# Sample attention and tail of a hybrid decoder kernel: serial loads, a second piece gathered ahead, two operands of the tail reloaded earlier

## The reference, cut to what matters

```
past_sel = gather_pages(cache_sel_kv, page_table)      # 8 samples x 2048 rows of k and v, 2 groups x 64
o_nsa = nsa_core(q, pos, cmp_kv, sel_kv, win_kv, ...)  # compressed, selected (top 16 blocks), window of 512
o_mem = mem_attend(qm, mem_kv)                         # 4 heads x 128 over 256 memory tokens
gates = sigmoid(g_br).reshape(B, T, 3, D_MODEL)        # g_br = columns of u @ w_in
merged = (gates[:, :, 0] * (o_nsa @ w_br_nsa) + gates[:, :, 1] * (o_gdn @ w_br_gdn)
          + gates[:, :, 2] * (o_mem @ w_br_mem))
h = x + merged @ w_out                                 # then the MLP on h
```

## Time and profile before

| | us |
|---|---|
| median of three runs | 1646.32 |
| lowest, highest | 1644.48, 1654.56 |
| the profiled execution's own time | 1644.59 |
| its span | 1642.8 |
| PE busy | 1453.0 (88%) |
| DVE busy | 871.7 (53%) |
| ACT busy | 384.5 (23%) |
| POOL busy | 82.1 (5%) |
| mean granted clock of PE | 0.929 |

### The profile page before, as it was taken

The page is one execution under the profiler, slowest core; times in us unless marked ns, Lnnn a source line. Parts: engine busy times, 40 slices in busy tenths (PEclk is TensorE's granted clock), DMA queues, the critical chain, the costliest instruction groups (busy, mean ns, idle before and its releaser), DMA issues. The chain is left out here.

```text
span 1642.8 us, 27036 instructions
## 1 busy us (share of the span) xinstructions
PE 1453.0 (88%) x11343; PEld 1335.0 (81%) x11343; DVE 871.7 (53%) x1590; ACT 384.5 (23%) x891; POOL 82.1 (5%) x76
## 2 busy tenths in 40 slices
PE   6999899889968788989475689999989999999998
PEld 5778789789957676878343489899988999999998
DVE  3555256747633565664233345545746746465563
ACT  3543023222233344554121221000003101000000
POOL 1000001100011111110100000000000000000000
PEclk8999999999968797999578789999999999999999
DMA  9232035251321000000538073323240332323221
GB/s 350 70 119 96 16 91 184 60 196 56 119 53 52 0 2 0 2 1 1 228 138 305 28 244 90 116 81 94 97 155 26 104 103 78 103 77 102 89 91 53
DMA packets 115648, 159.03 MB, mean 97 GB/s; under 512 B 6039, under 2 KB 106839, under 8 KB 112778
## 3 DMA queue, kind: packets, MB, share of 16 engines
q1 hardware_dynamic: 111886, 122.76, 23.4%
q0 software_dynamic: 2304, 33.56, 5.1%
q10 hardware_dynamic: 1348, 1.12, 0.2%
HBM read 145.04 MB, written 16.66 MB: 98 GB/s over the span
## 5 line engine op out<-in xcount | busy, mean ns | idle before, releaser
L330 PE MATMUL ps<-uH,wh 128*128 128x260 f32 x576 | 165.8, 288 | 12.3 <-DVE wt L301 9.0
L330 PE MATMUL ps<-hH,wh 128*128 128x260 f32 x512 | 145.3, 284 | 2.6 <-DVE hT L301 2.6
L330 PE MATMUL ps<-mergedH,wh 128*128 128x260 f32 x512 | 145.4, 284 | 0.0
L330 PE MATMUL ps<-hT,wh 128*128 128x260 f32 x512 | 145.3, 284 | 0.0
L330 PE MATMUL ps<-hH,wl 128*128 128x260 f32 x512 | 144.9, 283 | 0.0
L330 PE MATMUL ps<-mergedT,wh 128*128 128x260 f32 x512 | 144.7, 283 | 0.0
L330 PE MATMUL ps<-mergedH,wl 128*128 128x260 f32 x512 | 144.4, 282 | 0.0
L457 PE MATMUL ps<-XT,w 128*128 128x256 f32 (+1 forms) x512 | 125.5, 386 | 6.3 <-DVE XT L520 6.0
L330 PEld LDWEIGHTS ps<-uH,wh 128*128 128x128 f32 x576 | 109.9, 191 | 15.2 <-DVE wt L301 9.2
L330 PE MATMUL ps<-uL,wh 128*128 128x260 f32 x384 | 109.3, 285 | 0.0
L330 PE MATMUL ps<-uH,tw 128*128 128x260 f32 x384 | 109.0, 284 | 0.0
(11 more groups left out here) (520 smaller groups left out, 3437.1 us busy)
## 6 DMA issues: line engine op xcount, KB each, us to landing
wt<-in_w_ff SPq DMA_DIRECT2D x32, 1024.0 KB, 5.4
wt<-in_w_in SPq DMA_DIRECT2D x15, 1024.0 KB, 5.8
tw<-in_w_in SPq DMA_DIRECT2D x12, 1024.0 KB, 5.4
ring<-in_cache_mem_kv SPq DMA_DIRECT2D x4, 2048.0 KB, 25.0
w<-in_cmp_w SPq DMA_DIRECT2D x8, 512.0 KB, 6.3
ring<-in_cache_win_kv SPq DMA_DIRECT2D x2, 2048.0 KB, 19.5
out_s_win<-in_cache_win_kv SPq DMA_DIRECT2D x1, 4088.0 KB
scratch_uhigh<-uH SPq DMA_DIRECT2D x1, 2080.0 KB
```

Of the source, the lines that this page charges most:

```text
L330: ins = pe.matmul(out, lhsT(i, c), rhs(j, c), start=(first and c == 0 and k == 0), stop=(last and c == chunks - 1 and k == 2))
```

## The change

Four edits:

1. Sample 1's selected piece is gathered during the prompt mixers too, into `graw` (`self.ring_filled` becomes 2), on POOL behind the last group's "tv" on PE and "sc" on DVE. `graw` becomes slot 1 of the ring.
2. SP's window load and memory keys' load each wait until the piece before them in the order of use has landed (`wait_piece(sp, k - 1)`); the memory values' load does not.
3. When the second selected job has signalled `v_done`, SP reloads `uH`, `uL` and the tail's first weight tile `tw0` into slots 0, 2 and 3 of the ring, which are next to one another. The tail no longer loads them.
4. In the tail START becomes 5.0 instead of 13.0 and the first split's key 0.1 instead of 6.5, and the places of `tw1` and `s_S0` change.

```
@@ -1508,10 +1508,10 @@
 
         assert SEQ // 64 <= 16 and SEQ <= WIN
         nc, I, O, ps, proj = self.nc, self.I, self.O, self.ps, self.proj
-        self.ring_filled = 1
+        self.ring_filled = 2
         self.qmpad = self.sb_high("qmpad", [P, NB, MH, 32])
         self.compress_setup()
-        self.ring = [self.view("w1", [P, PAGES * 256], F32)]
+        self.ring = [self.view(x, [P, PAGES * 256], F32) for x in ("w1", "graw")]
         self.filled = [self.sem(f"e_slot{k}") for k in range(7)]
         XT, HT = self.sb("XT", [P, 4, SEQ // 2]), self.sb("HT", [P, 2, 2, PCMP])
         kc = self.sb("kcp", [P, NG, 32])
@@ -1807,6 +1807,10 @@
                 yield 42
                 pool.wait_ge(self.hid_ready, hid0 + 2)
                 self.gather_piece(pool, 0, 0)
+                yield self.delta_key(TT - 1, 2.5)
+                self.d_pe.wait(pool, "tv", TT - 1)
+                self.d_dve.wait(pool, "sc", TT - 1)
+                self.gather_piece(pool, 1, 1)
 
             @block.gpsimd
             def _(pool):
@@ -1822,7 +1826,9 @@
                 sp.dma_start(O["p_state"][0].rearrange("h k v -> k h v"), self.d["state"][:, :, :]).then_inc(stored, 16)
                 sp.wait_ge(stored, 16)
         self.free("w2", "hbias", "XT", "HT", "kcp", "vcp", "sc", "cs", "Pb0", "Pb1", "PTb0", "nm", "rs", "rg",
-                  "memhl", "qmT", "kmT", "mem_kv", "graw", *self.d_names)
+                  "memhl", "qmT", "kmT", "mem_kv", *self.d_names)
+        at, _ = self.taken.pop("graw")
+        self.taken["ring1"] = (at, at + PAGES * 256)
 
 
     def gather_piece(self, pool, b, n):
@@ -1857,6 +1863,14 @@
         sm, st = self.sb("sm", [P, 8]), self.sb("st", [P, 4])
         osb = [self.sb(f"osb{i}", [P, 512]) for i in range(2)]
         obr = ring[4][0:NB, 0:3 * NH * HD].rearrange("b (i c) -> b i c", i=3)
+        a, b = self.taken["w1"][0], self.taken["ring3"][1]
+        assert b - a == 3 * PAGES * 256 and self.taken["ring2"][0] == self.taken["w1"][1]
+        for name, n in (("uH", KC * NT), ("uL", KC * NT), ("tw0", KC * WCOLS)):
+            self.taken[name] = (a, a + n)
+            a += n
+        assert a <= b
+        self.uH, self.uL = (self.view(x, [P, KC, NT], F32R) for x in ("uH", "uL"))
+        self.tw0, self.u_back = self.view("tw0", [P, KC, WCOLS], F32), self.sem("t_u_back")
         scr = {n: nc.dram_tensor("scratch_" + n, (NB, 32, w), F32, kind="Internal").ap()
                for n, w in (("cmp", P), ("sel", P), ("win", P), ("mem", 512))}
 
@@ -2092,12 +2106,19 @@
                     if what == "sel":
                         continue
                     load_free(sp, k)
+                    if what != "memv":
+                        wait_piece(sp, k - 1)
                     if what == "win":
                         src = I["cache_win_kv"][4 * r:4 * r + 4].rearrange("b (t p) v g d -> p (b t) (v g d)", p=P)
                     else:
                         src = I["cache_mem_kv"][4 * r:4 * r + 4, :, 0 if what == "memk" else 1].rearrange("b (t p) h d -> p (b t) (h d)", p=P)
                     sp.dma_start(slot(k).rearrange("p (a c) -> p a c", a=src.shape[1]), src).then_inc(fetched[k % RING], 16)
 
+                sp.wait_ge(v_done, max(n for n, (br, _) in enumerate(jobs) if br == "sel") + 1)
+                for x, dram in zip((self.uH, self.uL), self.u_dram):
+                    sp.dma_start(x.bitcast(F32)[:, :, :], dram).then_inc(self.u_back, 16)
+                w0 = self.merge_tiles()[0][0][0]
+                sp.dma_start(self.tw0[:, :, :], w0.rearrange("(c p) n -> p c n", p=P)).then_inc(self.w_loaded[self.issued % 2], 16)
                 sp.wait_ge(c_scr, 16 * R4)
                 for k in range(2):
                     sp.wait_ge(o_scr[k], 16 * ((NJ - 1 + 1 - k) // 2))
@@ -2291,14 +2312,13 @@
         ident, cTs, acc, u0 = self.C("ident"), self.cTs, self.acc, self.units
         HB = GH * NB
         self.oH, self.oL = oH, oL = self.sbr("oH", [P, 3, 4, NT]), self.sbr("oL", [P, 3, 4, NT])
-        self.uH, self.uL = self.sbr("uH", [P, KC, NT]), self.sbr("uL", [P, KC, NT])
-        S0 = self.sb("s_S0", [P, GH, NB, P])
-        raw = [self.sb_high(f"tw{i}", [P, KC, W]) for i in range(3)]
+        raw = [self.tw0, self.sb("tw1", [P, KC, W]), self.sb_high("tw2", [P, KC, W])]
         low = [self.view(f"tw{i}", [P, KC, W], F32R) for i in range(3)]
         for i in range(2):
             self.sb_high(f"wh{i}", [P, KC, W])
         self.wh = [self.view(f"wh{i}", [P, KC, W], F32R) for i in range(2)]
         sig, prod2 = self.sb_high("sig", [P, 2, WM, NT]), self.sb_high("m_prod", [P, 2, HALF])
+        S0 = self.sb_high("s_S0", [P, GH, NB, P])
         at, _ = self.taken["proj"]
         self.taken["mergedT"], self.taken["mergedH"] = (at, at + KC * NT), (at + KC * NT, at + 2 * KC * NT)
         assert 2 * KC * NT <= TT * TOKCOLS
@@ -2330,7 +2350,7 @@
         tiles = [(gates if kind == "gate" else branches)[q] for kind, q in seq] + [(srcs, KC) for srcs in self.out_tiles()[0:2]]
         NT_, k0 = len(seq), self.issued
         assert k0 == self.splits == self.tiles
-        START = 13.0
+        START = 5.0
         start = [START]
         for kind, _ in seq:
             start.append(start[-1] + NU * (2.87 if kind == "gate" else 1.44))
@@ -2353,7 +2373,7 @@
 
         S = self.local_sem
         gated, taken, added = (S("m_" + x) for x in ("gated", "taken", "added"))
-        turned, oH_kept, oL_kept, u_back = (S("t_" + x) for x in ("turned", "oH_kept", "oL_kept", "u_back"))
+        turned, oH_kept, oL_kept = (S("t_" + x) for x in ("turned", "oH_kept", "oL_kept"))
         s_in, stored = S("s_in"), S("s_stored")
         p = Steps(S("s_pe"), ["sums", "bc", "qk", "read", "rows", "orow"] + [f"add{i}" for i in range(8)])
         a = Steps(S("s_act"), ["eg", "rt", "rows", "sqo", "ro"])
@@ -2377,9 +2397,6 @@
 
                 def loads():
                     yield 0.0
-                    load(0)
-                    for x, dram in zip((self.uH, self.uL), self.u_dram):
-                        sp.dma_start(x.bitcast(F32)[:, :, :], dram).then_inc(u_back, 16)
                     load(1)
                     for h in range(GH):
                         sp.dma_start(S0[:, h], I["state_gdn"][:, h].rearrange("b k v -> k b v")).then_inc(s_in, 16)
@@ -2411,7 +2428,7 @@
                             if i == 0:
                                 pe.wait_ge(self.w_split, k + 1)
                                 if n == 0:
-                                    pe.wait_ge(u_back, 32)
+                                    pe.wait_ge(self.u_back, 32)
                                 if kind == "branch" and q == 0:
                                     pe.wait_ge(oL_kept, EARLY)
                                 if kind == "branch" and q == BP:
@@ -2529,7 +2546,7 @@
                     self.high_low(dve, cut(raw[n % 3]), cut(self.wh[k % 2]), cut(low[n % 3]), self.w_high, k + 1).then_inc(self.w_split, 1)
 
                 def splits():
-                    yield 6.5
+                    yield 0.1
                     split(0)
                     for n in range(1, NT_ + 1):
                         yield start[n - 1] + 0.2
```

5 lines of the change are left out of this document (3 added, 2 removed).

## The result

Twenty runs of the changed kernel have a median of 1641.54 us (1634.36 to 1647.53), twenty of the kernel before 1650.74 (1644.48 to 1661.07): a ratio of 0.9939, 95% interval [0.9923, 0.9955]. The change is a gain of 0.6%, some 9 to 10 us. The forecast was 16.9 us off one profiled execution of 1644.59 us, 1628, with a range up to 1637. The measured median lies above that range.

A forecast was written before the change was run, and what follows sets the result against it. PE was taken as the bound, 88% busy, with waits for gathers in sample attention and for `uL` in the tail. Savings of 10.1 + 1.8 + 5.0 = 16.9 us off 1644.6 gave 1627.7, stated as 1628; range 1620 to 1637.

The forecast's parts named there:

- the base: Whole kernel: the one profiled execution, 1644.6 us, from which the summed gain was taken; median of runs put 1.7 above it.
- First job: Sample attention, first selected job: a piece gathered ahead and no loads beside the gathers save 10.1 us; bounds 5.2 and 11.1.
- Second job: Sample attention, second selected job: without the window load beside the gathers the last piece comes 1.8 us sooner; lower bound nothing.
- Rival C: Second selected job: engines serve both queues in turn, equal shares, so 5.2 us saved instead of 1.8; 1624.3; chance 0.08.
- rival D: Sample attention: each serial window or memory load comes late, 30.1 us lost against 16.9 won; 1657.8; chance 0.04.
- POOL's cover: Prompt mixers: the early gather's 0.94 us issue fits POOL's 18.08 us gap, costing nothing; 1.2 us if the cover were gone.
- one us in hand: End of sample attention: the reload ends at 932.4, read-backs went at 933.43, so no cost; bound a 2.6 us loss.
- The tail: Tail: the gate product starts earlier, without waiting for `uL`, saving 5.0 us; bounds nothing and 7.9.
- Rival B: Tail: the split at the head holds DVE and other work waits, so the tail gives nothing; 1632.7; chance 0.18.

The follow-up runs named there:

- after_again: An unchanged copy of the changed kernel, profiled and timed again: 1635.4 us, ratio to the kernel before 0.9900.
- no_ahead: The changed kernel without the second piece gathered in the mixers; serial loads and changed tail kept: 1641.5 us, ratio to the kernel before 0.9945.
- no_serial: The changed kernel with window and memory loads no longer waiting for the piece ahead of them: 1640.9 us, ratio to the kernel before 0.9928.
- win_early: The late_split kernel with the window load released by the selected job's third piece instead of the fourth: 1635.6 us, ratio to the kernel before 0.9897.
- before_again: An unchanged copy of the kernel before, profiled and timed again: 1650.3 us, ratio 0.9988.
- tail_only: The kernel before with only the changed tail and the reload; no early gather, no serial waits: 1647.5 us, ratio 0.9983.
- after_third: Another unchanged copy of the changed kernel: 1642.5 us, ratio to the kernel before 0.9935.
- late_split: The changed kernel with DVE's first gate-weight split behind the sample step's first operations and the third small product behind the first gate unit: 1635.5 us, ratio to before 0.9884.

## Why the prediction was wrong

**The sum's parts**, by the stages' means (before: two profiles, changed: three): g1 to g2 9.5 us, g2 to T 0.1, T to the end 3.4, together 12.9; forecast 16.9. So the terms were too large by 4 us, and the base was 6 us too low.

**The base is the step that failed most.** The prediction took 16.9 us off "the profiled execution", 1644.6, and set the median "1.7 above it", from three runs, without adding even these 1.7. Twenty runs put it 6.1 above. That execution had mixers of 341.7 us, where thirteen profiles reach to 352.8, and the difference goes with TensorE's clock. The whole mixers in the kernel before and in the changed kernel:

```profile
456.42:798.08 341.66, 282.29 (x1968) 247.62 (x1970) 183.31 (x434) 139.69 (x331) 47.62 (x39) 0.85 0.05 14
456.34:808.72 352.38, 293.66 (x1969) 257.01 (x1970) 183.08 (x434) 139.74 (x331) 48.50 (x40) 0.81 0.06 20
```

PE is busy 11.4 us longer at the lower clock, and stands idle as long: in all thirteen profiles the idle time of PE in the mixers is between 58.7 and 60.2 us, whatever their length. From 1650.7 the same sum gives 1633.8, still 7.7 us below the measured median. Why the clock differs between executions of one program no run shows. The account of the miss is 6.1 us of base, 4.0 of terms, and 3.7 between the stages' 12.9 and the medians' 9.2, less 0.3 of rounding: 13.5, the distance from 1628 to 1641.5. Of the 3.7 the pooled runs leave 1.7 with an uncertainty as large. Whether the early gather costs the mixers a part of that stays open: nine profiles with it have a mean of 348.6 us, four without it 346.5, and single profiles spread over 11.

**First job: 8.6 us, forecast 10.1.** The prediction reckoned 1.6 us to the first byte and then bytes at 401 GB/s, with PE starting at the last one. The trace shows a third stretch of time at the end. Windows of after_again, in which the first gather is issued at 801.95 and PE starts on the fourth piece at 815.58:

```profile
812.95:813.95 1.00, 0.18 (x1) 0.00 (x0) 0.69 (x1) 0.00 (x0) 0.00 (x0) 0.50 1.04 439
813.95:814.95 1.00, 0.00 (x0) 0.00 (x0) 0.00 (x0) 0.00 (x0) 0.00 (x0) 0.50 0.51 181
814.95:815.95 1.00, 0.37 (x2) 0.37 (x3) 0.00 (x0) 0.00 (x0) 0.00 (x0) 0.50 0.03 9
```

At the full rate the bytes would have been through at 814.4, 1.2 us ahead of PE. They are not: 256 of the 288 packets of two gathers have 16 KB (4.19 MB in all; the other 32 have 4 bytes, one for each engine and gather), and the 16 engines don't end together. The windows count a packet where it starts. Here are the gathers' packets that start from 814.38 on, in 814.5 to 814.6 (the last one of 16 KB), and from 814.6 to PE's start:

```profile
q0 software_dynamic: 11, 0.03, 6.8%
```

```profile
q0 software_dynamic: 1, 0.02, 38.2%
```

```profile
q0 software_dynamic: 7, 0.00, 0.4%
```

38.2% of 16 engines for 0.1 us is 0.61 us, so the last large packet, which starts at 814.55, ends at 815.16, and PE starts 0.42 us behind it. The end of a gather is thus some 0.8 us in which ever fewer engines still work, and 0.4 us from the last byte to PE. With 1.3 us for both, 1.6 at the start and 5.2 a piece, two pieces give 13.3 us, three 18.6, four 23.8; measured were 13.3 to 13.8, 19.0 (no_ahead), and 23.4 to 23.8. The Trainium skill, "DMA: Bandwidth & Descriptors", section "Anatomy of one DMA — SWDGE (gpsimd) path", gives a transfer's fixed cost as about 2 us and puts most of it behind the last byte, in the wait until that is confirmed as landed. The trace agrees in the sum, 1.7 us from the issue to the first packet and 0.4 from the last packet's end to PE, but not in where it lies.

The term was two: a piece ahead, forecast 5.2 and measured 5.3, and the loads kept away, forecast 4.9 and measured 3.2 to 3.4 (no_serial, no_ahead against before). Another 0.9 us came unasked between the fourth piece and g2: PE's clock is back at full between 16 and 20 us behind g1 (a mean of 0.86 over those four), before only at 28. Over the stretch from the fourth piece to g2 the mean clock was 0.78 before (35.1 us, of which 7.8 are lost by it) and 0.80 now (34.3 us, 6.9 lost), which is the 0.9. That the clock comes back sooner because the pauses in front of the pieces are fewer is not shown.

**Second job: 0.45 us, forecast 1.8.** The prediction counted 0.70 MB of loads ahead of the last piece. 0.13 MB of them were ACT's writes of small results, which stay. The DMA queues of the kernel before (packets, MB, share of 16 engines; q0 are the gathers, q1 SP's loads), from the first gather's issue to PE's start, and in the last 1.3 us of that:

```profile
q0 software_dynamic: 576, 8.39, 85.7%
q1 hardware_dynamic: 610, 0.62, 7.3%
```

```profile
q1 hardware_dynamic: 439, 0.45, 98.6%
q0 software_dynamic: 9, 0.02, 3.3%
```

Of 0.62 MB of loads 0.45 moved in these 1.3 us, on engines that were done with their part of the gathers (the last large packet ends at 879.20, 0.48 us ahead of PE). They held up next to nothing. Ahead were 0.17 MB, 0.43 us at 401 GB/s, close to the measured gain.

**Rival C was the right rule with the wrong weight.** It wanted equal shares and was said to agree with the trace "only if the gathers' packets are far larger than the loads'". They are: 16 KB against 1.0 KB. The queues of the kernel before in 804 to 816 us, with the loads beside the first job's gathers, and in 873.3 to 877.4 us, with the window load beside the second's:

```profile
q0 software_dynamic: 318, 4.69, 91.4%
q1 hardware_dynamic: 319, 0.33, 7.6%
```

```profile
q0 software_dynamic: 98, 1.57, 89.4%
q1 hardware_dynamic: 96, 0.10, 6.7%
```

The engines take turns: one packet of a load for one of a gather, which leaves the loads 6 to 7% of the two queues' bytes. That is why win_early cost almost nothing, and why the loads that move beside the first job's gathers are a small part of its 3.2 us. The Trainium skill, "DMA: Bandwidth & Descriptors", section "Queues, rings and completion order", says that each engine goes round the queues it has work for, a packet from each. The runs agree with it, one for one in the packets of the profile.

**Then why do the loads cost 3.2 us in the first job?** They are issued 0.7 us ahead of the gathers. The queues of no_serial in 809 to 814 us (the first gather is issued at 809.36), and from 814 to PE's start on the fourth piece, 826.3:

```profile
q1 hardware_dynamic: 1288, 1.32, 80.6%
```

```profile
q0 software_dynamic: 288, 4.19, 80.4%
q1 hardware_dynamic: 779, 0.81, 18.6%
```

Not one gathered packet moves in the first 4.6 us. In after_again, where nothing is ahead, the first one moves 1.7 us behind the issue at 801.95; its queues in 803.5 to 804.9:

```profile
q0 software_dynamic: 18, 0.29, 96.6%
```

That is 3.0 us of the 3.2. From their first packet to PE the gathers take nearly as long in both: 826.3 less 814.0, and 815.6 less 803.6, 12.3 and 12.0 us. (Both have something that the other lacks. In no_serial 0.40 MB of loads move beside the gathers, 0.41 more in the last 1.3 us; in after_again the first 0.29 MB take 1.4 us, 210 GB/s.) So once the gathers run, loads hardly disturb them. What costs is that with loads issued 0.7 us ahead the first gathered packet comes 4.6 to 4.7 us behind its issue, with 1.3 MB of loads gone before it, in all four profiles that have them so (before, before_again, no_serial, tail_only), and 1.7 us in the nine others. Turns packet by packet do not explain these 3.0 us, since by them the gathers would have their share from 1.7 us on: whether loads that are already queued must pass first, or the gathers' own start is held up beside them, no run separates. What counted was that the loads stood behind the gathers, not that each waited for a landing; that rests on the second job and on win_early. Loads issued without a wait just behind the first job's gathers were not tried. "Rules for kernel authors", on the same page of the Trainium skill, advises issuing early and waiting late. Here the early issue costs 3.2 us, where a later consumer's load goes ahead of the transfer that PE is waiting for.

**Serial loads late (rival D)**: no. They landed 9.7 us (window 0) and 13.5 (memory 0, the middle of keys and values) behind their issue, not 23.2 and 28.2, and no wait for them appears.

**POOL's cover** held: the early gather took 0.97 us at 716.88, and POOL idled 15.94 us behind it. Nearly unchanged is the end of sample attention: the read-backs go 77.3 to 78.3 us behind g2 in all but two of the thirteen profiles (78.9 and 79.5). The three without the reload have a mean of 77.6, the nine with all of it ahead 78.1, so "one us in hand" was right but for half a us, less than the profiles spread; and g2 to T did not grow.

**The tail: 3.4 us, forecast 5.0.** The start of the gate was sized rightly (7.6 us sooner, forecast 7.9), and so were the turns behind it (PE is busy 5.05 us with turns behind the gate's start, before 1.59: 3.5; forecast 3.7). The clock was not: the prediction allowed a loss of 0.3 us, and in the four us from the gate's start the mean was 0.67 in the first profile, a loss of 1.3 us, 0.96 in the next, and 0.61 in the third:

```profile
952.96:956.96 4.00, 4.00 (x25) 4.00 (x24) 3.84 (x4) 0.71 (x2) 0.00 (x0) 0.67 0.96 305
```

```profile
945.28:949.28 4.00, 4.00 (x35) 4.00 (x34) 3.84 (x4) 0.96 (x3) 0.00 (x0) 0.96 0.95 304
```

A wait of 0.85 us of PE for `mergedT`, 67 to 68 us behind T, is new as well; the prediction allowed 0.4 us for new waits. By the end of the tail's products the gain was 4.0, 5.0 and 3.7 us (the stage's last wait on PE, for `m_prod`, ends at T + 245.7 before, at T + 241.7, T + 240.7 and T + 242.1 now); at the end of the span it was 4.1, 3.1 and 3.0. So the first profile kept all of it, and the others gave back 1.9 and 0.7 us. In after_again some of this is PE's wait for `h`, 3.2 us against 1.8 and 1.5 in the two profiles of the kernel before (2.8 in after_third, 2.2 in the first), and some the clock, which drops once more behind that wait, where it was full before (a row of `--waits`, then the windows of after_again and of the kernel before at the same place):

```profile
PE ps L330 <- DVE h L2868: 3.2, 1, 3.2
```

```profile
1200.64:1206.64 6.00, 5.80 (x37) 4.36 (x38) 2.29 (x6) 0.00 (x0) 0.00 (x0) 0.72 0.61 178
```

```profile
1206.92:1212.92 6.00, 4.24 (x37) 3.77 (x37) 4.84 (x6) 0.00 (x0) 0.00 (x0) 1.00 0.48 147
```

The prediction took for granted that what moves the tail moves the end; it named no wait in the stage behind. Rival B (the tail gives nothing) is refuted, but its mechanism, the split holding the head of DVE's queue, was worth 3.0 us, as late_split shows (with the third small product moved too, and the clock's part in it). The forecast saw it and costed it; it didn't ask whether the split could stand four small operations further back.

## What to carry to other kernels

Before taking a predicted gain off a profiled time, ask where that execution lies among the kernel's runs, and compare stages rather than totals: here one stage spread over 11 us from execution to execution, and the rest repeated within 0.7. Time a transfer to the start of the one that waits for it, since its last packet on the slowest engine ends later than bytes over rate say, and don't count bytes that other engines move in between as ahead of it. Put a load that is wanted later behind the transfer that an engine waits for; once it stands behind, when exactly it starts matters little.

## What the runs showed of the hardware

- The prompt mixers, mixed work with short idle times on PE, took 341.6 to 352.8 us in thirteen executions of nearly the same program, in steps of 3 to 4 us, with a mean granted clock of 0.85 in the shortest and 0.81 in the longest and PE idle for 58.7 to 60.2 us in all of them.
- Gathers of 2.1 MB moved at 401 GB/s in packets of 16 KB, each 0.61 us on its engine. The first packet came 1.7 us behind the issue, and PE started 0.4 to 0.6 us behind the end of the last; since the engines did not end together, that was 1.2 to 1.3 us later than bytes over rate give.
- Beside gathers, loads with packets of 1.0 KB moved one packet for one gathered packet (319 to 318 in 12 us), 6 to 7% of the two queues' bytes.
- Loads issued 0.7 us ahead of gathers moved 1.3 MB first, and the gathers' first packet came 4.6 to 4.7 us behind its issue instead of 1.7, in four profiles against nine.
